# An encoder trunk with a mixture of experts on one core: GpSimd requests an expert's gathers ahead of the scatter of the expert four behind

## The reference

```python
e_global = g_idx * EXPERTS_PER_GROUP + e2
gates = jnp.einsum('tk,tke->te', p_g * w2, jax.nn.one_hot(e_global, N_EXPERTS))
for e in range(N_EXPERTS):                       # 32 experts, D 1024, FF 256
    y = (jax.nn.silu(t @ w_gate[e]) * (t @ w_up[e])) @ w_down[e]
    out = out + gates[:, e:e + 1] * y
```

## Time and profile before

| | us |
|---|---|
| median of 3 runs | 780.86 |
| lowest and highest | 780.75, 782.1 |
| the profiled execution's own time | 780.85 |
| its span, first to last instruction | 779.1 |
| TensorE matmul busy | 737.5 |
| VectorE, ScalarE, GpSimd busy | 297.1, 220.3, 201.2 |

### The profile page before, as it was taken

How to read it: one execution, slowest core, us unless ns; L and a number is a source line. 1 busy time by engine, 2 the same in 40 slices (tenths; PEclk the granted TensorE clock), 3 DMA queues, 4 the chain that set the end, 5 groups by cost and what they waited for, 6 DMA issues and landing times.

```text
span 779.1 us, 12116 instructions
## 1 busy us (share of the span) xinstructions
PE 737.5 (95%) x3886; PEld 408.2 (52%) x3887; DVE 297.1 (38%) x812; ACT 220.3 (28%) x595; POOL 201.2 (26%) x474
## 2 busy tenths in 40 slices
PE   8999999999888999998999998899997999999995
PEld 4555554444355666665455565455553555555542
DVE  2442211010188989983445455112111121112127
ACT  3643211101176777663111121011111011111123
POOL 1232422220024220330201133253342434342110
PEclk9999999999999999999999998999999999999999
DMA  9703003000140000000598427999999779999748
GB/s 345 277 0 109 0 1 108 1 0 1 42 181 1 2 1 1 2 1 1 201 424 321 163 83 259 377 413 415 415 416 416 268 275 409 419 415 406 275 155 345
DMA packets 36887, 154.64 MB, mean 198 GB/s; under 512 B 9652, under 2 KB 10804, under 8 KB 23904
## 3 DMA queue, kind: packets, MB, share of 16 engines
q1 hardware_dynamic: 28112, 136.50, 44.6%
q0 software_dynamic: 7504, 15.23, 5.3%
q10 hardware_dynamic: 1216, 2.23, 0.8%
HBM read 142.29 MB, written 20.03 MB: 208 GB/s over the span
## 4 chain that ended last, share of the span: by engine, by line
PE 82%; DMA 7%; issue 3%; POOL 3%; DVE 2%; ACT 2%; SPq 1%; POOLq 0%; DVEq 0%; ACTq 0%
PE banks L1534 20%; PE banks L1806 17%; PE banks L1690 9%; PE banks L1815 9%; PE banks L1606 4%; PE banks L1641 4%; PE banks L1797 3%; PE banks L1660 2%; PE banks L1615 2%; PE banks L1557 2%; DMA arena<-pair_rows 2%; PE banks L1664 2%; DMA arena<-h_rows,arena 2%; PE banks L1570 1%; PE banks L1560 1%
## 5 line engine op out<-in xcount | busy, mean ns | idle before, releaser
L1534 PE MATMUL banks<-arena 128*128 128x512 f32 (+1 forms) x384 | 162.1, 575 | 2.0 <-issue 1.6
L1806 PE MATMUL banks<-arena 128*64 128x256 f32 x1280 | 148.8, 385 | 2.8 <-DVE arena L1457 0.9
L1806 PEld LDWEIGHTS banks<-arena 128*64 128x64 f32 x1280 | 93.6, 138 | 50.8 <-issue 6.6
L1534 PEld LDWEIGHTS banks<-arena 128*128 128x128 f32 x384 | 71.5, 191 | 78.3 <-issue 78.3
L1690 PE MATMUL banks<-arena 128*128 128x512 f32 x192 | 86.4, 598 | 1.1 <-DVE arena L1277 1.1
L1815 PE MATMUL banks<-arena 128*64 128x512 f32 x320 | 79.8, 610 | 1.2 <-ACT arena L1068 0.9
L1232 DVE TENSOR_REDUCE arena<-banks 128x1 f32<-128x512 f32 (+1 forms) x96 | 55.4, 599 | 48.8 <-PE banks L1606 42.0
L989 ACT ACTIVATE arena<-banks,arena 128x512 f32<-128x512 f32 (+1 forms) x96 | 58.4, 614 | 43.2 <-DVE arena L1235 22.2
L1436 DVE TENSOR_TENSOR arena<-arena,banks 128x128 f32<-128x128 f32 x40 | 11.6, 290 | 151.3 <-ACT arena L1060 151.2
L1690 PEld LDWEIGHTS banks<-arena 128*128 128x128 f32 x192 | 35.1, 190 | 38.8 <-issue 37.5
L1060 ACT ACTIVATE arena<-banks 128x128 f32<-128x128 f32 x40 | 11.2, 279 | 153.6 <-PE banks L1806 153.6
(11 more groups left out here) (204 smaller groups left out, 900.1 us busy)
## 6 DMA issues: line engine op xcount, KB each, us to landing
arena<-w_gate SPq DMA_DIRECT2D x32, 1024.0 KB, 11.3
arena<-w_up SPq DMA_DIRECT2D x32, 1024.0 KB, 11.1
arena<-w_down SPq DMA_DIRECT2D x32, 1024.0 KB, 11.2
arena<-w_in SPq DMA_DIRECT2D x3, 2048.0 KB, 8.2
arena<-pair_rows SPq DMA_DIRECT2D x5, 1024.0 KB, 11.2
arena<-w_out SPq DMA_DIRECT2D x1, 4096.0 KB, 13.0
arena<-x SPq DMA_DIRECT2D x6, 512.0 KB, 10.2
residual<-arena SPq DMA_DIRECT2D x6, 512.0 KB, 7.1
```

Of the source, the lines that this page charges most:

```text
L1534: last = nc.tensor.matmul(bank(mm % 2)[:, 0:GROUP_COLS[g]], xgT[:, t, c, :], w[:, c, :], start=(c == 0), stop=(c == DC - 1))
L1806: last = nc.tensor.matmul(bank(b)[h * SLOTS:(h + 1) * SLOTS, 0:2 * P].rearrange("p (g n) -> p g n", g=2), x_eT[i][:, 2 * (c % 4) + c // 4, ...
```

## The change

In `rows_group` the scatter of expert e - 4 (`store_last`) moves from the start of step e to behind the two gathers, and stays ahead of `store_part` and the inner loop.

```diff
                 for s in members(g):
                     e = g * RING + s
-                    if s >= BEHIND:
-                        store_last(words, s - BEHIND, e - BEHIND)
-                    elif not isinstance(g, int) or g:
-                        store_last(words_before, s - BEHIND + RING, e - BEHIND)
                     n, before = extras(words, s)
                     with pool.If(n > 0):
                         await_count(e_xeT_psum, before + 1)
                         gather(EX, ids_sb, NE + e, e_id, before + 1)
                     if not isinstance(g, int) or e + AHEAD < NE:
                         gather_main(g, s + AHEAD)
+                    if s >= BEHIND:
+                        store_last(words, s - BEHIND, e - BEHIND)
+                    elif not isinstance(g, int) or g:
+                        store_last(words_before, s - BEHIND + RING, e - BEHIND)
                     if s:
                         store_part(words, s - 1, e - 1)
```

## The result

The changed kernel takes 788.79 us (median of 4 runs, 787.19 to 789.45), the kernel before 781.48 us in the runs beside it (780.75 to 783.39). The ratio is 1.0086, with a 95% interval of 1.0059 to 1.0114: **slower by 0.9%**, 7.3 us where 2.2 us were forecast. The profiled execution took 787.19 us, with a span of 785.4 us against 779.1.

A forecast was written before the change was run, and what follows sets the result against it. TensorE, busy 95% of the span, was taken as the bound, so only its waits count. Late buffers at experts 9, 13, 14, 15 and 19 (0.6 + 0.1 + 0 + 0.2 + 1.3) gave +2.2 us: 783.0 us, range 780.6 to 785.4.

The forecast's parts named there:

- plain experts: Experts without further rows: a late output buffer is covered there, lateness up to 3.6 us free.
- No gain from earlier gathers: Gathers issued 2.1 us earlier on GpSimd: TensorE's two gather waits, both in expert 13, stay untouched; gain 0.
- Expert 9: Scatter of expert 5 queued behind a buffer wait and two gathers, starting at 547.9: copy 0.6 us late (0.2 to 1.0).
- Rival 2: Scatters queue behind the gathers and land in 8.0 us: 5.8 us slower, 786.7 us; chance 0.08.
- Expert 13: Buffer 1.1 us late but absorbed in the following gather wait; 0.1 us charged for the portion's own scatter.
- Expert 14: Scatter starts at 611.0, its copy 7.6 us later, in a stretch with DMA share 0.47: 0 us.
- Expert 15: Scatter starts at 624.8, copy at 631.33, landing taken as 6.5 us: 0.2 us late (0 to 1.1).
- Expert 19: Scatter starts at 656.96, lands in 7.3 us, copy at 663.09: 1.3 us late (1.0 to 2.0).
- Rival 3: Shorter wait in expert 13 removes the clock's fall in 605 to 612 us: 1.6 us back, 779.3 us; chance 0.07.
- The queue of DMAs: Scatter landing times: measured median 7.0 us used, over the skill page's 2.6 us estimate, which would make the sum 0.
- Theory 4: Account from the experiments, not the prediction: the expert stage's shifted end puts the last products in a low clock, tail 33.5 us.

The follow-up runs named there:

- the other orders: Kernels with the scatter or gathers elsewhere in the step, or scatter one expert earlier, or moved in some slots only, against the kernel before: ratios from 1.0004 to 1.0284.
- the later one: The changed kernel run again, no edit, against the kernel before on the same chip: 786.61 us (8 runs), ratio 1.0064.
- the experiments on expert 14 alone: Scatter behind the gathers only in the third slot's steps (experts 2, 8, 14, 20, 26), otherwise the kernel before: 783.35 us, ratio 1.0041; further profiled runs 782.16 and 779.84 us.

## Why the prediction was wrong

The side was right, and so was the place of what the expert stage lost: the time went where the scatters that free the three output buffers come late, the moved gathers gave nothing, and plain experts covered their late copies (eight copies waited in the first profile; those of four experts without further work behind them cost nothing). The time of 783.0 us was wrong, and so was the range up to 785.4.

- **No gain from earlier gathers:** right. Both waits for a gather stayed (2.4 and 2.6 us).
- **Expert 9,** forecast 0.6, high end 1.0: 1.4 to 1.5 us in the first profile (a wait of 1.54, of which 0.1 was there before). The start was right to 0.1 us (547.9 on the old scale, against 549.83 with everything 1.9 us later). The time to landing was mis-sized: 8.0 us, where 7.0 was taken from neighbours of 6.6 and 7.4. Rival 2's 8.0 us came true here, though not at experts 15 and 19.
- **Expert 13,** forecast as absorbed: it was.
- **Expert 14,** forecast 0: *this is the step that failed.* The working gave it 7.6 us of margin and a quiet stretch of DMA (share 0.47). The margin held in three profiles of the change (7.7 to 7.9 us) and no wait came. The share was misread: the earlier trace rows has it for 605 to 612 us, but the scatter was to be under way from 611.0 to 618.6, and there it is 0.74 in the kernel before. The margin hangs on where the clock falls in expert 13: where it falls one portion earlier, it is 5.4 to 5.5 us, two weight loads are issued just ahead of the scatter, and the share while it has to land is 0.96 to 0.99. The wait was 3.3 and 3.0 us then, with 1.7 us of low clock behind it, a price that the sum has nowhere. The one execution from which all rows came did not show that form, and nothing in the working asked how the row of the clock might vary.
- **Expert 15,** forecast 0.2: 0.7 us (the copy came 7.2 us after the scatter's start, where 6.5 was taken for the landing; by its own figures the working should have had 0.1 here, and 1.0 at the high end instead of 1.1). **Expert 19,** forecast 1.3: 0.6 us (6.6 us where 7.3 was taken).
- **The sum** of 2.2 us is the expert stage's 2.4 in the form that the rows came from. In the other it is 6.5. The mean over five profiles each is 4.0 us. So of the 5.1 us by which the first comparison passed the forecast, the stage's mean, with the second form in it, accounts for 1.8; 1.1 us are the tail's, whose cause is open, and 0.2 the start's; for the remaining 2 us there is no profile, and single runs scatter by 10. The profiled execution of that comparison had the first form itself.
- **Rival 2,** at 786.7 us, is the nearest to the time, but by luck: it took 8.0 us for every landing because of the gathers ahead, with 0.5 us at expert 14 and 1.6 and 2.0 at experts 15 and 19, where 7.2 and 6.6 us were seen. Whether the gathers or the weight loads ahead stretched the landings at experts 9 and 14 no run separates; in each profile with the wait at expert 14 both stood ahead of the scatter or beside it.
- **Rival 3,** the clock, had the right subject, but its fall did not disappear: it is there in all five profiles of the change. It does come at another place at times and does give 1.2 to 1.7 us back, in the kernel before as well; in the changed kernel that same fall is what makes expert 14 late.
- **The queue of DMAs:** the scatters that came late landed in 6.6 to 8.6 us. The sentence of the Trainium skill, page "DMA: Bandwidth & Descriptors", section on the anatomy of a GpSimd DMA, on 2.0 us plus the bytes (an estimate of 2.6 us here) holds in these traces only where no weight load is under way, as the tail's 2.3 us shows, and 2.7 us for the changed kernel's gather of 611.85.

Left open: the tail. It is 33.4 us or more in four of five profiles of the change and in one of five before, always with the last eight products of line 1915 at 5.40 us instead of 3.70. That is 1.1 us in the mean. The long form has a somewhat longer wait for the loads ahead of it (1.87 to 2.02 us against 1.60 to 1.88), but five against five doesn't settle what brings it. Theory 4 fails as it was put: the second profile of the change has a short tail (31.6 us), the fourth of the kernel before a long one. The profiles of the other orders speak against it as well: all ten have the short tail (31.7 to 32.3 us), though the expert stage was as long in three of them (246.4 to 247.0 us) and 17 us longer in a fourth, and though the wait for those loads was up to 2.25 us. With 4.0 + 0.2 + 1.1 the ten profiles differ by 5.3 us in the mean. The first comparison's 7.3 us is higher, the later one's interval (2.3 to 7.7 us) holds it; the scatter of single runs, 10 us, doesn't allow more. For the experiments on expert 14 alone the mean time is known, but how often each form comes in unprofiled runs is not.

No kernel tried beats the one before beyond its interval. The scatter between the gathers equals it.

## What to carry over

Where a transfer frees a buffer, its margin is start plus time to landing against the next use, for each use; moving it behind other requests and behind their *waits* spends that margin, and a buffer that is late on an engine with no slack is paid in full. Take the margin not from one profile alone: see what in its stretch can vary (here the portion at which the clock falls) and work the step out for the other form too. And a wait has a second price where the clock falls behind it.

## What the runs showed of the hardware that had not been expected

- The granted clock falls at different places in executions of the same kernel: in the kernel before, in 604 to 612 us in three profiles and in 596 to 604 in two (0.79 or 0.80 in all). A portion that runs slow inside a wait that would have been there anyway costs nothing; as the next portion then ran at the full clock, the stage was 1.2 to 1.7 us shorter.
- Six waits of TensorE of 3.0 to 4.8 us before line 1815 were followed by the lower clock (1.97 to 1.98 us for the four down products); waits there of 0.4 to 2.8 us were not (1.08 us). The length of the wait alone doesn't decide elsewhere: in expert 13 the clock fell behind a first wait of 2.5 to 3.0 us in some profiles, and behind the second, after a first of 2.0 to 2.8 us, in others, and in the tail behind waits of 1.87 to 2.02 us in five profiles but not behind one of 2.25.
- The same indirect scatter of 128 rows lands in 2.3 us with the DMA engines nearly idle (share 0.08), and landed 8.6 us after its start where two weight loads of 1 MB had been issued 0.1 and 0.7 us ahead of it.
